# Norm statistics on all 128 partitions, the inverse by logarithm and exponential, and the layer norms' shift taken off the old residual

## The reference

```python
def rms_norm(x, g):
    y = xf * lax.rsqrt(jnp.mean(xf * xf, axis=-1, keepdims=True) + RMS_EPS)
    return (y * g).astype(x.dtype)
def layer_norm(x, g, b):
    mu = jnp.mean(xf, axis=-1, keepdims=True)
    var = jnp.mean(jnp.square(xf - mu), axis=-1, keepdims=True)
    return ((xf - mu) * lax.rsqrt(var + LN_EPS)) * g + b
# first layer
h = rms_norm(x, norm_mix_g); proj = h @ w_in      # three mixers, gated and merged
x = x + merged @ w_out
h = rms_norm(x, norm_ffn_g); u = causal_dwconv(h @ ffn_up, ...)
x = x + (gelu(u_gate) * u_val) @ ffn_down
x = rms_norm(x, final_norm_g)
# each of two layers
proj = x @ w_in                                    # pooling, windowed attention, gated conv
x = layer_norm(ALPHA * x + merged @ w_o, ln1_g, ln1_b)
x = layer_norm(ALPHA * x + (silu(a) * b) @ w_down, ln2_g, ln2_b)
```

## Time and profile before

| | |
|---|---|
| median of 3 runs | 1217.76 us (1217.31 to 1217.79) |
| the profiled execution | 1217.63 us, its span 1215.8 us |
| TensorE busy | 1199.6 us, 99% of the span |
| VectorE, ScalarE, GpSimd busy | 852.5, 707.5, 404.3 us |
| mean granted TensorE clock | 0.994 |
| chain that ended last | PE 89%, issue 4%, DVE 3%, POOL 3%, ACT 1% |

### The profile page before, as it was taken

The page is one execution under the profiler, slowest core; times in us unless marked ns, Lnnn a source line. Parts: engine busy times, 40 slices in busy tenths (PEclk is TensorE's granted clock), DMA queues, the critical chain, the costliest instruction groups (busy, mean ns, idle before and its releaser), DMA issues.

```text
span 1215.8 us, 27264 instructions
## 1 busy us (share of the span) xinstructions
PE 1199.6 (99%) x10242; PEld 1177.9 (97%) x10242; DVE 852.5 (70%) x1458; ACT 707.5 (58%) x1228; POOL 404.3 (33%) x376
## 2 busy tenths in 40 slices
PE   8999999999999999999999999999999999999997
PEld 8999999999999999999999999999999999999997
DVE  5868666676877755766678777656766678777655
ACT  5667667445766654466455666644566455666542
POOL 3007305123334302210339444314500339434313
PEclk9999999999999999999999999999999999999999
DMA  7655345654666665555654666664554554666562
GB/s 259 183 168 157 126 156 171 192 190 144 204 192 191 183 198 171 159 167 155 185 180 129 205 192 190 184 190 147 166 164 157 184 181 129 202 190 191 192 190 84
DMA packets 60288, 212.70 MB, mean 175 GB/s; under 512 B 6688, under 2 KB 7968, under 8 KB 60064
## 3 DMA queue, kind: packets, MB, share of 16 engines
q1 hardware_dynamic: 60192, 211.39, 56.5%
HBM read 210.31 MB, written 1.05 MB: 174 GB/s over the span
## 4 chain that ended last, share of the span: by engine, by line
PE 89%; issue 4%; DVE 3%; POOL 3%; ACT 1%; DMA 0%; POOLq 0%; DVEq 0%; ACTq 0%
PE bank L1065 28%; PE bank L1067 27%; PE bank L1066 27%; POOL acc L663 2%; PE bank L1206 1%; PE bank L1237 1%; PE bank L1122 1%; PE bank L1081 1%; DVE wlo L1391 1%; PE bank L1217 1%; POOL acc L659 1%; PE bank L1261 1%; ACT whi L735 0%; POOL u L650 0%; PE bank L1193 0%
## 5 line engine op out<-in xcount | busy, mean ns | idle before, releaser
L1391 DVE TENSOR_TENSOR wlo<-raw,whi 128x1024 fp32r<-128x1024 f32 (+1 forms) x400 | 490.4, 1227 | 216.2 <-ACT whi L735 213.9
L1065 PE MATMUL bank<-shifted,whi 128*128 128x256 f32 x2296 | 638.5, 278 | 1.4 <-POOL shifted L669 1.1
L1066 PE MATMUL bank<-shifted,whi 128*128 128x256 f32 x2296 | 636.0, 277 | 0.0
L1067 PE MATMUL bank<-shifted,wlo 128*128 128x256 f32 x2296 | 635.7, 277 | 0.0
L735 ACT ACTIVATE whi<-raw 128x1024 fp32r<-128x1024 f32 (+1 forms) x400 | 416.4, 1042 | 147.7 <-PE bank L1067 133.8
L1065 PEld LDWEIGHTS bank<-shifted,whi 128*128 128x128 f32 x2296 | 431.6, 188 | 2.8 <-POOL shifted L669 1.3
L1067 PEld LDWEIGHTS bank<-shifted,wlo 128*128 128x128 f32 x2296 | 431.7, 188 | 0.0
L1066 PEld LDWEIGHTS bank<-shifted,whi 128*128 128x128 f32 x2296 | 431.1, 188 | 0.0
L636 POOL TENSOR_TENSOR fprod<-ugate,uval 128x256 f32<-128x256 f32 x66 | 97.3, 1474 | 205.6 <-DVE uval L1739 183.3
L1065 PE MATMUL bank<-fhi,whi 128*128 128x256 f32 x528 | 145.8, 276 | 0.0
L1067 PE MATMUL bank<-fhi,wlo 128*128 128x256 f32 x528 | 145.8, 276 | 0.0
(11 more groups left out here) (212 smaller groups left out, 1245.1 us busy)
## 6 DMA issues: line engine op xcount, KB each, us to landing
raw<-in_w_win SPq DMA_DIRECT2D x140, 512.0 KB, 3.6
raw<-in_w_up SPq DMA_DIRECT2D x132, 512.0 KB, 3.5
raw<-in_w_down SPq DMA_DIRECT2D x48, 448.0 KB, 3.7
raw<-in_w_merge SPq DMA_DIRECT2D x32, 512.0 KB, 3.7
raw<-in_w_out SPq DMA_DIRECT2D x24, 512.0 KB, 3.5
raw<-in_w_down SPq DMA_DIRECT2D x24, 512.0 KB, 3.5
x<-in_x SPq DMA_DIRECT2D x4, 256.0 KB, 3.9
rgw<-in_rg_w SPq DMA_DIRECT2D x1, 1024.0 KB, 9.9
```

The costliest lines, as they stand in the source:

```text
L1065: pe.matmul(ps, whi[:, slot, w], hi, start=first, stop=False)
L1066: pe.matmul(ps, whi[:, slot, w], lo, start=False, stop=False)
L1067: return pe.matmul(ps, wlo[:, slot, w], hi, start=False, stop=last)
L1391: dve.tensor_tensor(wlo[:, n % RING, w], raw[:, n % RING, w], whi[:, n % RING, w].bitcast(f32), ALU.subtract) \
```

## The change

- **Sums.** `ones` is the stationary operand and the data the moving one, so each sum comes out on all 128 partitions as 128x256 in a bank. Diagonals, spreading matmuls and the statistics of 128x2 go. The order of the sources changes: in the first norm GpSimd's sum comes last; in layer norms the two sums over `acc` come first, then those over tile 7.
- **Mean and variance** are computed by VectorE on 128x256 (`mean_rows`, `var_rows`).
- **Inverse**: ScalarE takes a logarithm into `var_rows` and an exponential with scale -0.5 into the bank `inverse_rows`. `load_log` loads one table set explicitly in the places of `load_sqrt`.
- **Order**: the high part of the next stage's third unit goes behind the inverse in RMS norms (it was behind the root), and ahead of it in layer norms. In the first norm the low part of unit 0 moves from ahead of the scalings to between the second and the third.
- **Shift**: summed from tile 0 of the high part of the norm before, as a single-pass matmul within the ramp; ScalarE copies it into `acc[:, 0, :]` between its tiles 3 and 4; GpSimd adds it to the old `x`, one tile behind each of eight projection units (ln1) or every third product of the up stage, the eighth after its last product (ln2). The residual is then written straight to `dev`; `deviation` goes. VectorE waits for all eight shifted tiles at the head of wout and down.
- **Recentring**: VectorE takes two tiles, GpSimd six. At the end ScalarE writes all eight output tiles.
- **Dummies**: 9 instead of 12 behind an RMS norm's sum (10 instead of 11 at the first norm), 16 instead of 11 behind a layer norm's (none at the last one), 4 less ahead of a layer norm's sums.

```diff
+            def norm_inverse(which, eps):
+                ...
+                act.activation(var_rows, src, ACT.Ln, scale=scale, bias=eps_col(eps)).then_inc(logged, 1)
+                act.wait_ge(logged, SUM[which])
+                act.activation(inverse_rows, var_rows, ACT.Exp, scale=-0.5).then_inc(inverted, 1)
+            def load_log():
+                act.add_instruction(mybir.InstLoadActFuncSet(name=nc.get_next_instruction_name(), act_func_set_id=LN_AND_EXP))
+            def shift_copy(which):
+                act.wait_ge(shift_ready, LNI[which] + 1)
+                act.activation(shift_rows, shift_sum, ACT.Copy, scale=-1.0 / P).then_inc(shift_copied, 1)
...
@@ GpSimd, in the up stage of a layer
+                    if which is not None and i % 6 == 5:
+                        ...
+                        shift_x(which, i // 6, it)
                 repeat(pool, name, UPT, 6, body, peel_first=True)
+                if which is not None:
+                    shift_x(which, KT - 1)
                 low(FT - 1)
...
@@ TensorE
             def token_sums(dst, sources):
-                for h in range(2):
-                    for i, (src, ready, count) in enumerate(sources):
-                        if h == 0:
-                            pe.wait_ge(ready, count)
-                        mm = pe.matmul(dst[:, h:h + 1], src[:, h * P:(h + 1) * P], ones[:, 0:1], ...)
+                for i, (src, ready, count) in enumerate(sources):
+                    pe.wait_ge(ready, count)
+                    mm = pe.matmul(dst, ones[:], src, start=(i == 0), stop=(i == len(sources) - 1))
             def layer_norm(which, result):
                 released(result)
-                warm(4, result)
+                pe.wait_ge(added_d, (KT - 2) * (i + 1))
+                pe.matmul(dev_sums, ones[:], acc[:, 1, :], start=True, stop=False)
+                pe.wait_ge(added_q, ACCQ[which] + KT - 2)
+                pe.matmul(square_sums, ones[:], acc[:, 0, :], start=True, stop=False)
+                pe.wait_ge(res_new, RES[which] + KT)
+                pe.matmul(dev_sums, ones[:], dev[:, KT - 1, :], start=False, stop=True).then_inc(dev_summed, 1)
+                pe.wait_ge(dev_squared, KT * (i + 1))
+                pe.matmul(square_sums, ones[:], tmp[:, 3, :], start=False, stop=True).then_inc(summed, 1)
                 if which != NORMS[-1]:
-                    warm(8, result)
+                    warm(16, result)
@@ ramp
+                    if shift and (u, k) == (1, 0):
+                        pe.matmul(shift_sum, ones_hi[:], hi[0], start=True, stop=True).then_inc(shift_ready, 1)
...
@@ VectorE
             def layer_norm(which, last):
+                dve.tensor_scalar(mean_rows, dev_sums, -1.0 / DM, None, ALU.mult).then_inc(mean_ready, 1)
+                dve.wait_ge(mean_ready, i + 1)
+                dve.tensor_tensor(var_rows, mean_rows, mean_rows, ALU.mult).then_inc(mean_squared, 1)
                 dve.wait_ge(mean_squared, i + 1)
                 dve.wait_ge(summed, SUM[which])
+                dve.scalar_tensor_tensor(var_rows, square_sums, 1.0 / DM, var_rows, ALU.mult, ALU.subtract).then_inc(var_ready, 1)
+                for t in range(RECENTRED_BY_DVE):
+                    dve.tensor_tensor(dev[:, t, :], dev[:, t, :], mean_rows, ALU.add).then_inc(recentred_dve, 1)
+                dve.wait_ge(inverted, SUM[which])
             def down(name, which, alpha):
                 if which in LNI:
-                    dve.wait_ge(x_kept, KT * LNI[which])
+                    dve.wait_ge(x_shifted, KT * (LNI[which] + 1))
```

More of the change, by code:

```diff
@@ L186, in schedule @@
             at(b + 14 + 4 * pair + (pair == 2), "values", w)
+        for t in range(KT):
+            at(b + 18 + t, "shift_x", l, t)
         at(b + 14, "pool_sums", l)
@@ L619, in steps, with ffn @@
                         STEPS[name](*a)
-            def ffn(f, name):
+            def ffn(f, name, which=None):
                 def low(t, it=0):
@@ L770, in norm_shift @@
                         .then_inc(normed_act if last else x_hi, 1)
+                    if t == 3 and which in NEXT:
+                        shift_copy(NEXT[which])
             def norm_hi(which, src, after={}):
@@ L777, in norm_hi @@
                     act.activation(xhi[t], src[:, t, :], ACT.Copy).then_inc(x_hi, 1)
+                    if t == 3 and which in NEXT:
+                        shift_copy(NEXT[which])
+            act.wait_ge(ones_set, 1)
+            act.activation(ones_hi[:], ones[:], ACT.Copy).then_inc(ones_copied, 1)
             act.wait_ge(prep, 1)
-            load_sqrt()
+            load_log()
             for t in range(0, KT, 2):
@@ L978, in body @@
                         hi_part(n + 2, it, 6)
-                    if i % 3 == 1 and not (isinstance(it, int) and i < 6):
+                    if which in LNI and i % 3 == 0 and not (isinstance(it, int) and i == 0):
+                        square(which, i // 3 - 1, it)
+                    if which not in LNI and i % 3 == 1 and not (isinstance(it, int) and i < 6):
                         square(which, i // 3 - 2, it)
@@ L1087, in _, with ramp @@
             LATER = [(u, k) for u in range(2) for k in range(5)] + TOGETHER[10:]
-            def ramp(n, result, ready, order=TOGETHER, split=(xhi, xlo)):
+            def ramp(n, result, ready, order=TOGETHER, split=(xhi, xlo), shift=False):
                 hi, lo = split
@@ L1318, in body @@
                         if i == 0:
-                            ramp(n, r, lows(which))
+                            ramp(n, r, lows(which), shift=which in NEXT)
                         return
@@ L1358, in _ @@
                 name = f"win2{l}"
-                ramp(START[name], RESULT[name], lows("ln20" if l else "final"))
+                ramp(START[name], RESULT[name], lows("ln20" if l else "final"), shift=True)
                 for p, (kind, t) in enumerate(PLAN2):
@@ L1721, in wout @@
                         lo_part(START[name] + t + 2)
[L1722 to L1727 removed]
+                    residual(name, t, START[name] + t, alpha, bank_of(RESULT[name] + t), which)
             def up(f, name, cols, width):
```

226 lines of the change are left out of this document (83 added, 143 removed).

## The result

After: **1209.68 us** median of 4 (1209.33 to 1209.97), against 1217.68 of the kernel before beside it (1217.31 to 1217.79); ratio 0.9931, 95% interval 0.9919 to 0.9943. The profiled execution took 1209.73 us (span 1207.9), so 7.9 us less than the profiled one of before. Forecast were 9.7.

A forecast was written before the change was run, and what follows sets the result against it. TensorE was taken as the bound, with no gap except at seven norms. The terms 0.45 + 0.73 + 0.5 + 5.2 + 1.26 + 1.8 - 0.2 = 9.7 us gave 1208.0 us, range 1205.3 to 1212.8.

The forecast's parts named there:

- Layer norms: Three norms between stages: inverse by mean, square, variance, logarithm, exponential; first scaling 1.8 us earlier; 5.2 us gained in all.
- "ffn": RMS norm: logarithm and exponential replace root, diagonal and spreading; first product at 296.1 against 296.86, 0.73 us gained.
- "final": RMS norm like "ffn", less 0.2 us because the shift's copy stands between high parts 3 and 4: 0.5 us gained.
- the end: Last layer norm and output: earlier scaling, GpSimd recentring six tiles instead of seven, last transfer at 1211.3: 1.8 us gained.
- the down product's wait: VectorE's new wait for eight shifted tiles: 0.74 us late at worst, taken as 0.1 each, 0.2 for two layers.
- the earlier residual: Inner layer norms: tile 7's residual starts at 648.32, with no deviation in front, and is the deviation itself.
- First norm: Start of the kernel: diagonal and spreading saved, weight splits eat part; 0.45 us gained (0 to 1.0).
- rival B: TensorE's clock falls to half as products begin, losing 1.5 us at three of six norms: 1212.5 us; chance 0.10.
- The prediction's own sign of being wrong: Wrong if the clock is half in a ramp, VectorE's recentring exceeds 0.9 each, or down-product split waits exceed 1 us.
- The shift's sums: Four f32 sums of 0.43 us leave TensorE's full stretch for single-pass ones in ramps: 1.26 us gained.
- Rival A: VectorE and GpSimd contend: mean's square and recentrings 0.95 us each, 0.74 lost per down product; 1213 us; chance 0.15.
- Rival C: Table loads of 1.283 us in every norm's path: 1226 us with two, 1217 with one; chance 0.06.

The follow-up runs named there:

- best_residual_twice: best_candidate with tile 7's residual made in two dependent steps in each layer norm, into x and then copied into dev: 1206.71 us.
- best_candidate: The kernel after with 18 first-norm dummies, VectorE's shifted-tile wait behind the second weight split of each down product, and the eighth shift behind GpSimd's last low part: 1206.61 us.

## Why the prediction was right, and where it was not

The forecast was 1208.0 us and 1209.68 were measured, inside the range. Part by part:

- **Layer norms, "ffn", "final", the end: right, by the forecast chain, with some luck.** -1.95, -2.09 and -1.79 were measured for -1.92, -2.02 and -2.02, and -0.87 for -0.73. At ln10 and ln11 the near hit is in part luck: the ramps gained 2.0 each, more than forecast, and the down product's wait took it back (below). The forecast had left the stretch from the first scaling to the fifth low part as it was (654.19 to 658.93); it is now 652.48 to 656.99, so 0.23 shorter. VectorE's first four low parts in it took 0.61, 0.56, 0.56 and 0.57 before, beside GpSimd's recentring up to 658.3, and take 0.47, 0.56, 0.57 and 0.47 now that this ends at 655.6. That is read from the rows; no run tests it alone.
- **Inside a layer norm** the inverse came 0.29 later than forecast (652.24 for 651.95), as tile 7's sum starts at 649.30 and not at 648.97: the sum over `acc` ahead of it waits for GpSimd's addition (it starts at 648.77, forecast 648.54). It cost nothing, since VectorE's recentring held the scaling to 652.48, which the forecast had at 652.4. And the deviation that is no longer made gains next to nothing at two of three inner norms (best_residual_twice): the sums of 0.43 cover it. The prediction had put those sums in front, and yet told of the earlier residual as a step of the gain.
- **First norm: wrong by 2.1 us.** The step that failed is the sentence on rival B, "at the first one the gap is 2.3 us, but VectorE paces it there". VectorE and GpSimd pace that ramp to 18.69 only; the half clock came behind it. Here the gap in front of the starved ramp was paid at the ramp's end. The 0.45 counted for the arithmetic came out as 0.18. The sum began at 9.38, 0.69 behind the last square, and was to begin with it: the step that has the copy of the ones end before x is there left out the 18 dummies queued behind that copy. The rival was right in kind and price (1.5) and was named at the wrong norms: the inner ones kept 1.00, with a gap of 0.4 behind the dummies where I had worked out 1.15. With 2 dummies they lose 0.8 to 2.2 each. The prediction's own sign of being wrong, half clock in a ramp, did come.
- **The down product's wait: mis-sized,** 0.79 each for 0.1. GpSimd's product did become 0.61 faster without the split beside it, as granted, but the split became 0.53 longer beside GpSimd's low part, a term that the prediction had at nothing. With the worst case of 0.74 the sum would have been 1.3 nearer.
- **The shift's sums: right in sum, not place by place.** Counted from the end of the ramps, before to best_candidate (the wait mended), the stages behind "final", ln10, ln20 and ln11 fall by 0.17, 0.75, 0.02 and 0.54, so 1.48 in all, for four times 0.43 forecast. The stage behind "final" alone differs by up to 0.4 among the kernels here (164.12 to 164.53), so single stages say little.
- **Rival A** came in part. On the mean's square it did not: 0.42 although GpSimd starts 0.05 behind it. VectorE's recentrings took 0.49 and 0.95 (two in 1.36), between the ends. Its loss in the down products did come (0.79 for 0.74). By the rule of the Trainium skill cited in the prediction the square would have cost 0.95; the trace does not agree there and does for one of the two recentrings.
- **Rival C** did not come, thanks to the explicit load alone.

## What to carry to other kernels

Dummy matmuls are part of a kernel's schedule: an edit that shortens or moves a wait must recount them up to the first product that TensorE takes without waiting, and the granted clock is to be read behind the ramp too, not only in it. When a wait is added to an in-order engine, price it by what is queued behind it, at full, until a row shows who gives the time back. Before counting a removed operation as gained, ask what else its reader waits for.

## What the runs showed of the hardware

- VectorE and GpSimd, both with two SBUF inputs and 0.04 to 0.06 us apart: either VectorE took 0.96 for 0.42 or GpSimd 1.06 for 0.74. The same instructions came out both ways in different kernels. A weight's split (128x896) took 1.61 for 1.08 beside a GpSimd low part; a GpSimd low part took 2.08 for 0.74 beside VectorE's work in the first ramp.
- ScalarE's activation from PSUM or into it costs 0.47 and 0.39 for 128x256, from SBUF 0.51.
- Start-up varies in kernels with the same transfers. The last tile of x was squared between 6.96 and 8.55 us. The first dummies ran at half rate (0.43 us each) up to a moment between 3.9 and 8.4 us and at full rate (0.22) behind it, and the sum waits for the later of x and the dummies: in best_residual_twice x was there at 7.02 and the sum came at 9.06, behind the dummies. In the kernels that kept the full clock in the first ramp the last product ahead of "ffn" came between 290.13 and 291.21.
